# Three reorderings in a two-block sequence kernel: a weight piece converted one step earlier, a residual loaded in four parts, and two projections swapped

## The chip, the cores and the metric

One NeuronCore of a Trainium2 chip runs the whole program in one launch. The metric is device microseconds, lower is better. The kernel before takes 1913.19 us (median of three runs, 1912.94 to 1916.48).

## The reference

The input is 512 tokens of width 1024. The first block runs two layers; each layer scales and shifts its input by a conditioning vector, projects it, runs two recurrent branches (HGRN2 and RWKV7) beside a gate projection, merges them and adds a residual. The second block is one RG-LRU layer and one retention layer. What the change touches is this (cut down):

```
for l in range(2):                                   # first block
    y_hg = o_hg @ w_branch_hg[l];  y_rw = o_rw @ w_branch_rw[l]
    merged = y_hg * sigmoid(gate[0:1024]) + y_rw * sigmoid(gate[1024:2048])
    x = layer_norm(DN_ALPHA * x + (1 + ...) * (merged @ w_out[l]))   # the layer residual x
# RG-LRU layer of the second block
xb = conv4(h @ w_x) + b ;  gate = h @ w_g            # 12 blocks of 128 columns each
a, u = gates(xb);  hseq = scan(a, u);  y = hseq * silu(gate)
```

## The kernel before

Everything is kept transposed, channels on 128 partitions and the 512 tokens along the free dimension. All weights are one list of **pieces** (231 of them, 512 KB each: eight 128x128 tiles). A product in 32 bit is made of three matmuls on rounded parts, so each piece goes through a fixed chain:

- SyncE (SP) loads it into one of two raw buffers (`load_block`, L571), when GpSimd is done with the piece two before it;
- ScalarE (ACT) makes the rounded part `w_hi` (`weights(b)`, L806), when the load has landed and TensorE has used piece b-2;
- GpSimd (POOL) makes the rest `w_lo`, in two instructions of 128x512 (L719);
- TensorE (PE) multiplies, 24 matmuls a piece (L2344 for one output tile, L2363 for four side by side).

Activations are split likewise: a **high part** on ACT (`high`, L814, which waits until VectorE has made the source) and a low part on VectorE (DVE; `low`, L1405). PE waits for both before it uses a tile. The order on each engine is written by hand; each engine works through its own list in order, and semaphores tie the lists together.

**The branch stage** (once for each of the two layers) has eight pieces, b_br to b_br+7: four for the HGRN2 output and four for the RWKV7 output, two pieces for each half of the output columns. PE handles a piece in two steps. Its step for the third RWKV7 tile waits for the low part of that tile and for the first half of w_lo of piece b_br+5, the sixth. DVE makes the four RWKV7 tiles in `normed_head(j)` (four instructions each, L1405 and L1843); `normed_head(3)` also holds the low part of tile 2. ACT meanwhile makes four sigmoids of the gates (`gates(n)`, L1113, 128x2048 each). DVE then scales the residual (L1878) before `merge(0)`; PE's results of the first RWKV7 half are read there. SP loads the 4 MB of gates and then the 2 MB residual x.

**The RG-LRU stage** starts with four convolved blocks x0 to x3, projected side by side into four PSUM banks; after that every block (x for a convolved one, g for a recurrent gate one) goes in turn into one of two PSUM banks, proj0 and proj1, in the order of `LRU_ORDER`. PE may start block n only when the bank of block n-2 has been read. An x block is read by a plain copy on ACT into one of two staging buffers, and DVE convolves it from there (one TENSOR_SCALAR at L1996, three SCALAR_TENSOR_TENSOR at L1408). A g block is read last by DVE: ACT makes its sigmoid into the staging buffer (L1204), and DVE multiplies that with the bank (L1405), which frees it. `staged_before` makes ACT wait until the staging buffer has been convolved.

## Time and profile before

| what | value |
|---|---|
| median of three runs | 1913.19 us (1912.94 to 1916.48) |
| the profiled execution | 1914.83 us, span 1913.0 us |
| PE busy | 1826.5 us, 95% of the span |
| DVE busy | 1101.1 us, 58% |
| ACT busy | 816.8 us, 43% |
| POOL busy | 702.3 us, 37% |
| mean granted TensorE clock | 0.982 |

The span is the time between the first and the last recorded instruction; the execution's own time is 1.83 us more. All times in rows are microseconds from the start of the span unless marked ns.

### The profile page before, as it was taken

What the parts mean: (1) busy time and instruction counts of PE and PEld (TensorE: products, weight loads), DVE (VectorE), ACT (ScalarE), POOL (GpSimd) and SP (SyncE); (2) the same over time, 40 slices, a digit from 0 to 9 for tenths busy, and PEclk for the clock granted to TensorE, in tenths of its full rate; (3) what the DMA queues carried; (4) which work ended last, traced back from release to release, by engine and by line L of the source; (5) the groups of instructions that cost most, each with busy time, mean ns of one, the idle gap of its engine ahead of it and who ended that gap; (6) DMA issues with size and microseconds to landing.
All of it is one profiled execution on the core that took longest, in us unless ns stands there. A gap on an engine that the chain in (4) does not pass through costs nothing.

```text
span 1913.0 us, 35599 instructions
## 1 busy us (share of the span) xinstructions
PE 1826.5 (95%) x14714; PEld 1453.3 (76%) x14714; DVE 1101.1 (58%) x1431; ACT 816.8 (43%) x1173; POOL 702.3 (37%) x488
## 2 busy tenths in 40 slices
PE   7999999999998999999999997899998999999996
PEld 4778877899775877777899784775676888888875
DVE  7775787633455118787633453658845446546454
ACT  2343645533533443755533534345724324323332
POOL 2454433210252435643210251333453435343332
PEclk9998999999998999999999999999998999999998
DMA  9782222200431522222200432322143322222222
GB/s 366 237 258 71 88 95 93 80 26 4 166 99 44 172 83 83 88 94 89 84 26 4 166 99 88 143 67 66 56 143 123 108 60 84 67 78 72 71 99 99
DMA packets 63201, 193.24 MB, mean 101 GB/s; under 512 B 5936, under 2 KB 6192, under 8 KB 62672
## 3 DMA queue, kind: packets, MB, share of 16 engines
q1 hardware_dynamic: 63056, 191.10, 30.3%
q8 instruction: 116, 1.90, 0.4%
q14 instruction: 29, 0.24, 0.0%
HBM read 173.25 MB, written 17.83 MB: 100 GB/s over the span
## 4 chain that ended last, share of the span: by engine, by line
PE 62%; issue 21%; DVE 7%; POOL 7%; ACT 2%; DMA 0%; POOLq 0%; SPq 0%; DVEq 0%; ACTq 0%
PE proj L2344 39%; POOL w_lo_sb L719 6%; PE aux L2363 4%; PE aux L2602 3%; DVE slots_sb L1405 2%; PE proj L2602 1%; PE aux L2517 1%; PE aux L2659 1%; DVE area_sb L1405 1%; PE aux L2656 1%; PE aux L2962 1%; PE aux L2968 1%; PE aux L2374 1%; PE aux L2959 1%; DVE slots_sb L1408 1%
## 5 line engine op out<-in xcount | busy, mean ns | idle before, releaser
L719 POOL TENSOR_TENSOR w_lo_sb<-w_raw_sb,w_hi_sb 128x512 fp32r<-128x512 f32 x462 | 684.6, 1503 | 1033.3 <-ACT w_hi_sb L806 1033.2
L2344 PE MATMUL proj<-act_hi_sb,w_hi_sb 128*128 128x512 f32 x1480 | 604.0, 408 | 14.9 <-POOL w_lo_sb L719 3.4
L2344 PE MATMUL proj<-act_hi_sb,w_lo_sb 128*128 128x512 f32 x1480 | 579.3, 391 | 0.0
L2344 PE MATMUL proj<-act_lo_sb,w_hi_sb 128*128 128x512 f32 x1480 | 578.3, 391 | 0.0
L806 ACT ACTIVATE w_hi_sb<-w_raw_sb 128x1024 fp32r<-128x1024 f32 x231 | 244.5, 1058 | 673.0 <-PE proj L2344 516.2
L2344 PEld LDWEIGHTS proj<-act_hi_sb,w_hi_sb 128*128 128x128 f32 x1480 | 279.1, 189 | 98.3 <-issue 30.6
L2344 PEld LDWEIGHTS proj<-act_lo_sb,w_hi_sb 128*128 128x128 f32 x1480 | 279.4, 189 | 63.0 <-issue 8.9
L2344 PEld LDWEIGHTS proj<-act_hi_sb,w_lo_sb 128*128 128x128 f32 x1480 | 278.9, 188 | 60.1
L2363 PE MATMUL aux<-act_hi_sb,w_hi_sb 128*128 128x512 f32 x336 | 137.7, 410 | 23.3 <-issue 18.2
L1405 DVE TENSOR_TENSOR area_sb<-area_sb 128x256 f32<-128x256 f32 (+1 forms) x180 | 117.7, 698 | 44.4 <-PE aux L2518 28.2
L2363 PE MATMUL aux<-act_lo_sb,w_hi_sb 128*128 128x512 f32 x336 | 133.5, 397 | 0.0
L2363 PE MATMUL aux<-act_hi_sb,w_lo_sb 128*128 128x512 f32 x336 | 133.4, 397 | 0.0
L1405 DVE TENSOR_TENSOR slots_sb<-slots_sb 128x512 f32<-128x512 f32 (+1 forms) x67 | 84.4, 1262 | 42.3 <-ACT slots_sb L1109 22.6
L1405 DVE TENSOR_TENSOR slots_sb<-proj,const_sb 128x512 f32<-128x512 f32 x44 | 30.4, 691 | 118.5 <-PE proj L2344 118.2
L2363 PEld LDWEIGHTS aux<-act_hi_sb,w_hi_sb 128*128 128x128 f32 x336 | 65.0, 193 | 42.6 <-issue 24.5
L1405 DVE TENSOR_TENSOR area_sb<-area_sb,slots_sb 128x512 f32<-128x512 f32 (+1 forms) x90 | 83.5, 946 | 17.8 <-ACT slots_sb L828 11.3
L2363 PEld LDWEIGHTS aux<-act_lo_sb,w_hi_sb 128*128 128x128 f32 x336 | 64.9, 193 | 15.1 <-issue 1.9
L2363 PEld LDWEIGHTS aux<-act_hi_sb,w_lo_sb 128*128 128x128 f32 x336 | 64.6, 192 | 13.9
L2659 PE MATMUL aux<-area_sb 64*64 64x64 f32 x1280 | 71.9, 218 | 0.4 <-issue 0.2
L2602 PE MATMUL aux<-area_sb 64*64 64x64 f32 x1792 | 68.8, 219 | 3.1 <-issue 2.1
L1408 DVE SCALAR_TENSOR_TENSOR slots_sb<-proj,derived_sb,stage_sb 128x512 f32<-128x512 f32 x24 | 18.0, 751 | 93.2 <-ACT stage_sb L876 93.2
L2602 PEld LDWEIGHTS aux<-area_sb 64*64 64x64 f32 x1792 | 63.8, 135 | 4.3 <-issue 2.7
(310 smaller groups left out, 2557.8 us busy)
## 6 DMA issues: line engine op xcount, KB each, us to landing
w_raw_sb<-wall SPq DMA_DIRECT2D x231, 512.0 KB, 3.6
area_sb<-w_ada SPq DMA_DIRECT2D x32, 512.0 KB, 4.5
slots_sb<-w_ada SPq DMA_DIRECT2D x32, 256.0 KB, 6.9
gate_scr<-stage_sb SPq DMA_DIRECT2D x32, 256.0 KB, 2.2
area_sb<-gate_scr SPq DMA_DIRECT2D x8, 1024.0 KB, 9.7
x_scr<-area_sb SPq DMA_DIRECT2D x3, 2048.0 KB, 7.7
area_sb<-x_scr SPq DMA_DIRECT2D x2, 2048.0 KB, 13.5
area_sb<-lru_gates SPq DMA_DIRECT2D x1, 3584.0 KB, 11.7
```

The lines of the kernel that those rows point to most:

```text
L719: nc.gpsimd.tensor_tensor(w_lo[:, b % 2, :, :].rearrange("p k n -> p (k n)")[:, half], w_raw[:, b % 2, half], w_hi[:, b % 2, :, :].rearran ...
L806: A(w_hi[:, b % 2, :, :].rearrange("p k n -> p (k n)"), w_raw[:, b % 2, :], ACT.Copy)\
L1405: return TT(out_ap, a, b, op)
L1408: return STT(out=out_ap, in0=in0, scalar=scalar, in1=in1, op0=op0, op1=op1)
L2344: ins = MM(bank, w[:, s, k, :], a[:, t, :], start=(start and i == 0), stop=(stop and i == len(terms) - 1))
L2363: ins = MM(bank, w[:, s, 4 * (k % 2) + i, :], a[:, t, :], start=(k == 0 and n == 0), stop=(k == len(tiles) - 1 and n == 2))
L2374: return nc.tensor.transpose(dst, src, C("ident"))
L2517: MM(x[0:64, early], a[:, early], b[:, early], start=True, stop=True)
L2602: ins = MM(x[q, columns * j:columns * j + columns], a[q, j, :], b(q, j), start=(i == 0), stop=(i == len(products) - 1))
L2656: MM(x[q, 64 * j:64 * j + 64], xt[q, j, :], z[q, j, :], start=True, stop=True)
L2659: ins = MM(x[q, at:at + 64], z[q, j, :], xt[q, j, :], start=True, stop=True)
L2959: ins = MM(x, r_vtok[:, c, vs], r_scores[:, cols], start=True, stop=(c == 0))
```

## The change

Three orders are changed; no arithmetic is.

1. ACT converts piece b_br+5 before it makes the high part of RWKV7 tile 3, in both layers.
2. The residual of each layer is loaded in four parts of 512 KB. Ahead of each part stands the load of one more weight piece (b_br+4 to b_br+7), so a part can be issued only when that piece's raw buffer is free. DVE waits for all four parts where it waited for the one load.
3. The list of RG-LRU blocks begins with g0, x4 instead of x4, g0, on ACT, DVE and PE, and in the order of the pieces.

```
-LRU_ORDER = [("x", 4), ("g", 0), ("g", 1), ("x", 5), ("g", 2), ...
+LRU_ORDER = [("g", 0), ("x", 4), ("g", 1), ("x", 5), ("g", 2), ...
...
                 src = x_scr[0] if l else dram["x_t"]
-                sp.dma_start(xa[:, :, :], src.rearrange("k p t -> p k t")).then_inc(S("x_in"), 16)
+                for i in range(4):
+                    blocks_to(b_br + 5 + i)
+                    sp.dma_start(xa[:, 2 * i:2 * i + 2, :], src[2 * i:2 * i + 2].rearrange("k p t -> p k t"))\
+                        .then_inc(S("x_in"), 16)
...
                 high_rw(2)
+                weights(b_br + 5)
                 high_rw(3)
-                weights(b_br + 5)
                 gates(2)
                 gates(3)
...
-                dve.wait_ge(S("x_in"), 16 + 16 * l)
+                dve.wait_ge(S("x_in"), 64 + 64 * l)
...
+            lru_block("g", 0)
             lru_block("x", 4)
-            lru_block("g", 0)
             lru_block("g", 1)
```

The last piece of the diff stands on ACT and on DVE, and PE's list begins likewise; later waits on `x_in` count the six additional loads.

**On ACT in the branch stage**, from the high parts of tiles 0 and 1 (first row) to the conversion of piece b_br+7 (last row). L806 and L809 are `weights`, L814 and L817 `high`, L1113 and L1116 `gates`. Before:

```order
L814 ACTIVATE act_hi_sb<-slots_sb 128x512 [waits split_src] x2
L806 ACTIVATE w_hi_sb<-w_raw_sb 128x1024 [waits block_used,raw_in1]
L1113 ACTIVATE area_sb<-area_sb 128x2048 [waits gate_in1]
L814 ACTIVATE act_hi_sb<-slots_sb 128x512 [waits split_src] x2
L806 ACTIVATE w_hi_sb<-w_raw_sb 128x1024 [waits block_used,raw_in0]
L1113 ACTIVATE area_sb<-area_sb 128x2048 [waits gate_in2]
L1113 ACTIVATE area_sb<-area_sb 128x2048 [waits gate_in3]
L806 ACTIVATE w_hi_sb<-w_raw_sb 128x1024 [waits block_used,raw_in1]
L806 ACTIVATE w_hi_sb<-w_raw_sb 128x1024 [waits block_used,raw_in0]
```

The same place of the changed kernel, up to the last gates:

```order
L817 ACTIVATE act_hi_sb<-slots_sb 128x512 [waits split_src] x2
L809 ACTIVATE w_hi_sb<-w_raw_sb 128x1024 [waits block_used,raw_in1]
L1116 ACTIVATE area_sb<-area_sb 128x2048 [waits gate_in1]
L817 ACTIVATE act_hi_sb<-slots_sb 128x512 [waits split_src]
L809 ACTIVATE w_hi_sb<-w_raw_sb 128x1024 [waits block_used,raw_in0]
L817 ACTIVATE act_hi_sb<-slots_sb 128x512 [waits split_src]
L1116 ACTIVATE area_sb<-area_sb 128x2048 [waits gate_in2]
L1116 ACTIVATE area_sb<-area_sb 128x2048 [waits gate_in3]
```

The conversion stands between the two high parts now; the gates and the conversion of b_br+6 still come behind the second of them.

**On SP behind the loads of the gates** in layer 0, the changed kernel has these rows; L571 is `load_block`, L680 a part of the residual:

```order
L675 DMA area_sb<-gate_scr 128x4x512 x3
L571 DMA w_raw_sb<-wall 128x1024 [waits lo_ready]
L680 DMA area_sb<-x_t 128x2x512
L571 DMA w_raw_sb<-wall 128x1024 [waits lo_ready]
L680 DMA area_sb<-x_t 128x2x512
L571 DMA w_raw_sb<-wall 128x1024 [waits lo_ready]
L680 DMA area_sb<-x_t 128x2x512
L571 DMA w_raw_sb<-wall 128x1024 [waits lo_ready]
L680 DMA area_sb<-x_t 128x2x512
```

Before, the row behind the gates was one load of x, 128x8x512, which waited for nothing, and the weight loads followed.

**On DVE at the start of the RG-LRU blocks**, from the convolution of x3 on. L1996 with L1408 x3 is one convolution, a L1405 with `proj` among its inputs frees the bank of a g block. Before:

```order
L1996 TENSOR_SCALAR slots_sb<-stage_sb,vec_sb 128x512 [waits aux_read3]
L1408 SCALAR_TENSOR_TENSOR slots_sb<-stage_sb,vec_sb,slots_sb 128x512 [waits dve_chain] x3
L1996 TENSOR_SCALAR slots_sb<-stage_sb,vec_sb 128x512 [waits proj_read1]
L1408 SCALAR_TENSOR_TENSOR slots_sb<-stage_sb,vec_sb,slots_sb 128x512 [waits dve_chain] x3
L1405 TENSOR_TENSOR slots_sb<-proj,stage_sb 128x512 [waits sig_staged] x2
```

And in the changed kernel, where the same helpers stand three lines further down:

```order
L1999 TENSOR_SCALAR slots_sb<-stage_sb,vec_sb 128x512 [waits aux_read3]
L1411 SCALAR_TENSOR_TENSOR slots_sb<-stage_sb,vec_sb,slots_sb 128x512 [waits dve_chain] x3
L1408 TENSOR_TENSOR slots_sb<-proj,stage_sb 128x512 [waits sig_staged]
L1999 TENSOR_SCALAR slots_sb<-stage_sb,vec_sb 128x512 [waits proj_read0]
L1411 SCALAR_TENSOR_TENSOR slots_sb<-stage_sb,vec_sb,slots_sb 128x512 [waits dve_chain] x3
L1408 TENSOR_TENSOR slots_sb<-proj,stage_sb 128x512 [waits sig_staged]
```

The multiplication for g0 stands between the convolutions of x3 and x4 now. The first bank of the blocks belongs to g0 instead of x4, so it is freed by this DVE instruction, where ACT's copy of x4 freed it before.

## Rows read from the trace of the kernel before

**Rows 1.** The page, busy time of each engine.

```profile
PE 1826.5 (95%) x14714; PEld 1453.3 (76%) x14714; DVE 1101.1 (58%) x1431; ACT 816.8 (43%) x1173; POOL 702.3 (37%) x488
```

**Rows 2.** Timeline, PE, branch stages: start, duration, work, idle before and its releaser.

```profile
523.46 0.39 PE L2363 MATMUL aux<-act_hi_sb,w_lo_sb 128*128 128x512 f32 x1
525.68 0.50 PE L2363 MATMUL aux<-act_hi_sb,w_hi_sb 128*128 128x512 f32 x1 [1.83 <-POOL w_lo_sb L719]
...
531.25 0.39 PE L2363 MATMUL aux<-act_hi_sb,w_hi_sb 128*128 128x512 f32 x1
...
1099.90 0.50 PE L2363 MATMUL aux<-act_hi_sb,w_hi_sb 128*128 128x512 f32 x1 [1.45 <-POOL w_lo_sb L719]
```

**Rows 3.** Timeline, ACT, branch stage of layer 0.

```profile
519.45 0.64 ACT L814 ACTIVATE act_hi_sb<-slots_sb 128x512 fp32r<-128x512 f32 x1 [3.43 <-DVE slots_sb L1405]
522.69 0.63 ACT L814 ACTIVATE act_hi_sb<-slots_sb 128x512 fp32r<-128x512 f32 x1 [2.60 <-DVE slots_sb L1405]
523.23 1.04 ACT L806 ACTIVATE w_hi_sb<-w_raw_sb 128x1024 fp32r<-128x1024 f32 x1
524.18 3.71 ACT L1113 ACTIVATE area_sb<-area_sb 128x2048 f32<-128x2048 f32 x2
527.79 1.05 ACT L806 ACTIVATE w_hi_sb<-w_raw_sb 128x1024 fp32r<-128x1024 f32 x1
```

**Rows 4.** Timeline, POOL, branch stage of layer 0.

```profile
509.05 1.29 POOL L719 TENSOR_TENSOR w_lo_sb<-w_raw_sb,w_hi_sb 128x512 fp32r<-128x512 f32 x1 [6.64 <-ACT w_hi_sb L806]
...
524.35 1.28 POOL L719 TENSOR_TENSOR w_lo_sb<-w_raw_sb,w_hi_sb 128x512 fp32r<-128x512 f32 x1 [7.51 <-ACT w_hi_sb L806]
...
528.91 1.29 POOL L719 TENSOR_TENSOR w_lo_sb<-w_raw_sb,w_hi_sb 128x512 fp32r<-128x512 f32 x1 [2.03 <-ACT w_hi_sb L806]
```

**Rows 5.** Timeline, DVE, branch stage of layer 0.

```profile
509.12 1.76 DVE L1405 TENSOR_TENSOR slots_sb<-slots_sb 128x512 f32<-128x512 f32 x1
...
521.24 0.69 DVE L1405 TENSOR_TENSOR slots_sb<-slots_sb 128x512 f32<-128x512 f32 x1
...
522.58 0.68 DVE L1405 TENSOR_TENSOR act_lo_sb<-slots_sb,act_hi_sb 128x512 fp32r<-128x512 f32 x1
...
526.36 2.67 DVE L1878 TENSOR_SCALAR area_sb<-area_sb 128x4096 f32<-128x4096 f32 x1
```

**Rows 6.** Timeline, SP: issues of x and of piece b_br+7.

```profile
492.02 2.17 SPq L678 DMA_DIRECT2D area_sb<-x_t  x1
...
527.06 0.33 SPq L571 DMA_DIRECT2D w_raw_sb<-wall  x1
```

**Rows 7.** The page, DMA issues: count, KB each, us from issue to landing.

```profile
w_raw_sb<-wall SPq DMA_DIRECT2D x231, 512.0 KB, 3.6
...
area_sb<-x_t SPq DMA_DIRECT2D x1, 2048.0 KB, 17.4
```

**Rows 8.** Timeline, PE, the first matmuls of g1 and of x5.

```profile
1234.35 0.47 PE L2344 MATMUL proj<-act_hi_sb,w_hi_sb 128*128 128x512 f32 x1 [2.56 <-ACT stage_sb L1202]
...
1242.65 0.47 PE L2344 MATMUL proj<-act_hi_sb,w_hi_sb 128*128 128x512 f32 x1 [0.96 <-DVE slots_sb L1405]
```

**Rows 9.** Timeline, ACT, the RG-LRU stage.

```profile
1233.61 0.60 ACT L1202 ACTIVATE stage_sb<-proj 128x512 f32<-128x512 f32 x1 [2.15 <-DVE slots_sb L1408]
```

**Rows 10.** Timeline, DVE: convolution of x3, then the multiplication of g0.

```profile
1233.44 1.48 DVE L1996 TENSOR_SCALAR slots_sb<-stage_sb,vec_sb 128x512 f32<-128x512 f32 x1
...
1235.74 1.65 DVE L1408 SCALAR_TENSOR_TENSOR slots_sb<-stage_sb,vec_sb,slots_sb 128x512 f32<-128x512 f32 x1
...
1241.82 0.68 DVE L1405 TENSOR_TENSOR slots_sb<-proj,stage_sb 128x512 f32<-128x512 f32 x1
```

**Rows 11.** Windows, PE: window, length, busy (instructions), granted clock, DMA share, GB/s.

```profile
1235.20:1238.60 3.40, 3.40 (x10) 0.51 0.51 154
...
1371.90:1375.00 3.10, 3.06 (x7) 0.50 0.24 34
...
1181.80:1187.60 5.80, 5.80 (x8) 0.52 0.00 0
```

More of the change, by code:

```diff
@@ L35 @@
 RET_LOG = [math.log(1.0 - 2.0 ** (-5.0 - h)) for h in range(RET_HEADS)]
-LRU_ORDER = [("x", 4), ("g", 0), ("g", 1), ("x", 5), ("g", 2), ("x", 6), ("g", 3), ("x", 7), ("g", 4), ("x", 8),
+LRU_ORDER = [("g", 0), ("x", 4), ("g", 1), ("x", 5), ("g", 2), ("x", 6), ("g", 3), ("x", 7), ("g", 4), ("x", 8),
              ("x", 9), ("g", 5), ("x", 10), ("g", 6), ("x", 11)] + [("g", j) for j in range(7, 12)]
@@ L2039, in low_y @@
                 low(SPLITS["lru_y"] + t, (t + 8) % RT, G_S[:, t, :])
+            lru_block("g", 0)
             lru_block("x", 4)
-            lru_block("g", 0)
             lru_block("g", 1)
@@ L2117, in _ @@
             dve.wait_ge(S("rms_rs"), 2)
-            dve.wait_ge(S("x_in"), 48)
+            dve.wait_ge(S("x_in"), 144)
             def ret_low(m):
@@ L2317, in _ @@
                 evacuated(dve, RET_OUT + KT + m)
-            onto_x(1, "post1", 8, 112, S("x_final"))
+            onto_x(1, "post1", 8, 208, S("x_final"))
         @block.tensor
@@ L2866, in lru_blocks @@
                     used(project(lru_piece(half, j)))
-            lru_blocks(("x", 4), ("g", 0), ("g", 1), ("x", 5), ("g", 2), ("x", 6))
+            lru_blocks(("g", 0), ("x", 4), ("g", 1), ("x", 5), ("g", 2), ("x", 6))
             pe.wait_ge(S("lru_w"), 16)
```

## The prediction

> **What bounds the kernel now.** I read the page first: TensorE (PE) is busy 95% of the span [rows 1]. So an edit is worth what it takes from or adds to the moments in which PE stands still, and I went through PE's timeline at the three places. In the branch stage PE waits once in each layer, 1.83 us in layer 0 and 1.45 us in layer 1, both times for GpSimd's half of `w_lo` of piece b_br+5 [rows 2]. At the start of the RG-LRU blocks it waits 2.56 us before g1, for ACT's copy of x4, and 0.96 us before x5, for DVE's multiplication of g0 [rows 8]. Behind the first of these waits the granted clock is 0.51 for 3.4 us, that is the lower level, 1.2 GHz for 2.4 [rows 11]. Work behind each place starts from PE, so I let a shift there run through to the end.
>
> **Part 1, the earlier conversion.** ACT makes the high part of tile 2 at 519.45, and has to wait until 522.69 for the source of tile 3; the conversion of b_br+5 follows at 523.23, 0.54 later, and GpSimd begins at 524.35, 1.12 later still [rows 3, 4]. In the new order the conversion starts at 519.45 + 0.54 = 519.99 and GpSimd at 521.11. The first half of w_lo would be there by 522.4, before PE gets to its step: PE's last matmul ahead of the wait starts at 523.46 [rows 2]. By that alone the whole wait goes.
>
> But PE's step also needs the low part of tile 2, which DVE makes at the end of `normed_head(3)`, from 522.58 for 0.68 [rows 5]. Now GpSimd works beside that head. Its price is in the trace: a DVE TENSOR_TENSOR with both inputs in SBUF that starts at 509.12, just behind a GpSimd subtraction of 509.05 for 1.29, takes 1.76 us; one with nothing beside it (521.24) takes 0.69 [rows 4, 5]. The first of the head's last two multiplications starts at 521.24, 0.13 behind GpSimd's new start, and the second meets the second subtraction. Each is 1.07 longer, together 2.1. The low part then starts at 524.7 and is done at 525.4, and PE starts at about 525.4, where it started at 525.68. Of 1.83 us some 0.3 is gained.
>
> The Trainium skill (SBUF — State Buffer, section on the port rules for engines) states that VectorE and GpSimd share a port pair as an exclusive lock, that a VectorE instruction with two SBUF inputs is blocked by a GpSimd one that reads SBUF, and that it is blocked for the whole of it. The 1.76 us agree with that.
>
> Then comes what stands behind the late high part of tile 3. It waits for that head and moves from 522.69 to 524.8. The two gates follow 0.54 later, at 525.33, and take 3.61 to the next conversion [rows 3]; b_br+6 is converted at 528.94 instead of 527.79, and GpSimd begins on it at 530.06 instead of 528.91 [rows 4]. PE's two steps took from 525.68 to 531.25, 5.57 us [rows 2], so now they end at 530.97, and the next step needs GpSimd's first half: 530.06 + 1.29 = 531.35 with nothing beside it. That is 0.15 us later than 531.25, the lower bound.
>
> The upper bound comes from the scaling of the residual on DVE. It stood at 526.36 for 2.67, of which some 2.15 is its own, since GpSimd's two subtractions from 524.35 end at about 526.9 [rows 4, 5]. All of DVE is 2.1 later, so it starts at 528.5 if x is there, ends at 530.65 and, if a GpSimd instruction waits as long as a DVE one does, holds the first half of b_br+6 until 531.9: PE 0.7 later. This comes again in layer 1, where the wait is the same one [rows 2].
>
> **Part 2, the residual in four loads.** Before, x was issued at 492.02 and landed 17.4 us later, at 509.4, so 17 us before DVE wants it [rows 6, 7]. It hid completely, and no weight load was late for it: ACT's conversions there wait for none. The split can gain nothing. Now the last part stands behind the load of b_br+7, which waits for GpSimd to finish b_br+5. That was issued at 527.06 [rows 6]; with GpSimd 2.9 earlier (its second half waits for DVE once) it is about 524.4, and the last part of x goes out at 524.8. A load of 512 KB lands after 3.6 us [rows 7], which is 528.4; with the weight load ahead of it on the same engines, 6 MB in some 20 us being 1.7 us for 512 KB, it is 530.1. DVE wants it at 528.5. If x comes at 529.3, the middle, the scaling ends at 531.45, and GpSimd's half at 532.7: PE 1.5 later. At worst x comes just ahead of GpSimd's start, the scaling runs from 530.0 to 532.15, and PE is 2.2 later; if it comes after, GpSimd is first and the loss falls to 0.2 to 0.7. I take 1.3 us for each layer, between 0.7 and 1.5 but nearer to the latter as x is likelier late than not. Both layers: +2.6 (0.3 to 4.4). Extra issues on SP, 0.33 each [rows 6], delay no load that is waited for.
>
> **Part 3, g0 ahead of x4.** PE may start g1 when the bank of the first block is read. Before, that was ACT's copy of x4 at 1233.61, which only had to wait for the convolution of x2 [rows 9]. Now it is DVE's multiplication of g0, behind the convolution of x3. That one begins at 1233.44; its TENSOR_SCALAR takes 1.48 beside GpSimd, and its second SCALAR_TENSOR_TENSOR, from 1235.74, takes 1.65 [rows 10] where it would take 0.75 alone (an estimate: two more such instructions in the same convolution differ by the same 0.9 us with and without GpSimd). GpSimd comes 1.3 later here, since ACT loads the sigmoid's table and makes g0's sigmoid ahead of that conversion. So the second takes 0.75, to 1236.5, and the third meets GpSimd's start within some hundredths: it ends at 1237.3, or at 1238.35 if GpSimd is first. With 0.68 for the multiplication [rows 10] PE starts g1 at 1238.1 or 1239.2, instead of 1234.35 [rows 8].
>
> From there to x5, before: 1242.65 - 1234.35 = 8.3, of which 1.7 is the low clock (3.4 us at half speed, [rows 11]) and 0.96 the second wait [rows 8]; 5.6 is the block itself. After: the second wait is gone, as the bank of x4 is read by then. PE has stood still for over 6 us, and I expect the clock at its lower level when it starts. After other long waits it stayed there for 3.1 and for 5.8 us of work [rows 11]; half of that is 1.55 to 2.9, and I take 2.0. So x5 starts at 1238.1 + 5.6 + 2.0 = 1245.7 or at 1246.8, that is 3.0 or 4.1 later. I take +3.3; bounds 2.6 and 5.0.
>
> The Trainium skill (TensorE: Matmul & The Clock Gate, "HAM oscillation — how this bites in real kernels") warns that waits of PE between groups of matmuls put the array back at its low clock, so that a wait costs more than its length. The 0.51 behind 2.56 us of waiting agrees.
>
> **Sum.** 2.6 + 3.3 = 5.9 us. On the profiled execution's own time, 1914.83, that is 1920.7. That execution is 1.64 above the median of the three, 1913.19, so against the median it is 1919.1.
>
> **The rivals.**
> - *No measurable change* (24%). The POOL subtraction wins against the scaling in both layers and x is not late (+0.2 each, or a gain of 0.3 each), and the RG-LRU term is at its low end, 2.6: 1915 to 1917. For it: these are orders of a few hundredths. Against it: the clock, which has fallen in every longer wait that I looked at.
> - *Faster* (6%). The wait in the blocks is only moved: DVE works without a break for long stretches later in the RG-LRU stage, and a stall shared with those would be paid once. The delay is then taken up, the second wait and the low clock are gone (0.96 + 1.7), and the conversion gives both waits in full (1.83 + 1.45): -5.9, 1907.3. It decides if x5 starts no later than 1242.65. Against it: g1 cannot start before the convolution of x3 ends, and 1237.3 + 5.6 is past 1242.65 without any low clock.
> - *Slower by more* (in the 70% for slower, about 12%). PE's new wait for b_br+6 passes 2.5 us in both layers, and the clock falls there as it did behind 2.56 us: 1.7 more each, 1922.5 to 1924.
> - *The conversion does what it says* (within the others, 15%): if DVE's head is not held, the waits go in full, -3.3, and with the RG-LRU term nothing is left: 1913.2.
>
> **How the numbers follow.** Forecast 1919.1, slower by 0.31%. What a measurement of this kernel can tell from no change is 0.2%, 3.8 us. Terms at their bounds give +2.9 to +9.4; with the case of unheld heads the lower end reaches 1913.2, of which I leave out the last part: 1914.5 to 1923.0. Faster 0.06, same 0.24, slower 0.70.
>
> **What would show it.** Part 1: PE's wait for `w_lo` before tile 3 replaced by a shorter one for DVE's `act_lo`, two multiplications of 1.7 us on DVE, and a new PE wait of 1 to 2 us some 5.5 us later. Part 2: DVE's scaling preceded by a wait for the x DMA. Part 3: a single PE wait of 6 to 7 us before g1, and none before x5. I am wrong if DVE and GpSimd do not hold each other there, or if the clock comes back at once.

## The result

The changed kernel took 1921.27 us (median of 7 executions, 1918.9 to 1922.03), the kernel before in the same session 1913.78 us (7 executions, 1911.55 to 1917.35). The ratio is 1.0031, with a 95% interval of 1.002 to 1.0042: slower by 0.3%, about 6 us. The two medians themselves lie further apart, 7.5 us or 0.39%, which is inside that interval.

**Stretch by stretch.** The two profiled executions span 1913.0 and 1920.2 us (the latter is the slowest of its seven), and I cut both at six moments that exist in each. The timeline of PE after the change has them as follows (start, duration, work, idle before and its releaser): the first matmul of the branch stage of layer 0, the end of that stage in the layer norm, the same two of layer 1, the first matmul of the RG-LRU stage, and the first behind a wait that stands late in that stage.

```profile
489.31 1.13 PE L2771 MATMUL aux<-slots_sb,const_sb 128*128 128x512 f32 x2 [0.48 <-ACT slots_sb L1040]
...
600.79 0.70 PE L2803 MATMUL aux<-area_sb,const_sb 128*128 128x512 f32 x1 [0.91 <-DVE area_sb L1411]
...
1065.42 0.70 PE L2771 MATMUL aux<-slots_sb,const_sb 128*128 128x512 f32 x1 [0.48 <-ACT slots_sb L1040]
...
1173.49 1.10 PE L2388 MATMUL aux<-stage_sb,const_sb 128*128 128x512 f32 x2 [1.54 <-ACT stage_sb L824]
...
1201.37 0.58 PE L2366 MATMUL aux<-act_hi_sb,w_hi_sb 128*128 128x512 f32 x1 [5.02 <-issue]
...
1325.02 0.47 PE L2347 MATMUL proj<-act_hi_sb,w_hi_sb 128*128 128x512 f32 x1 [1.60 <-DVE slots_sb L1408]
```

Before, these moments were 489.47, 599.13, 1064.06, 1168.77, 1197.02 and 1317.78; the wait at the last of them was 1.60 us there too. The differences give this table, in us. All later ones are in it as well, so that each experiment can be read from it; "change" is the kernel with all three parts.

| kernel | branch 0 | between | branch 1 | between | RG-LRU | rest | span |
|---|---|---|---|---|---|---|---|
| before | 109.66 | 464.93 | 104.71 | 28.25 | 120.76 | 595.22 | 1913.0 |
| after (the change) | 111.48 | 464.63 | 108.07 | 27.88 | 123.65 | 595.18 | 1920.2 |
| e1, part 1 alone | 110.42 | 464.93 | 105.43 | 27.51 | 120.36 | 595.15 | 1909.9 |
| e2, part 2 alone | 109.75 | 466.14 | 104.73 | 27.67 | 120.50 | 595.14 | 1913.4 |
| e3, part 3 alone | 109.69 | 465.60 | 105.01 | 27.97 | 123.70 | 595.26 | 1920.0 |
| e4, change, no collision | 108.90 | 464.69 | 104.17 | 27.42 | 124.80 | 595.13 | 1917.4 |
| e5, part 1, next piece earlier | 109.38 | 465.81 | 104.41 | 28.41 | 120.84 | 595.07 | 1915.4 |
| e7, both convolved blocks first | 111.30 | 465.78 | 105.06 | 27.50 | 119.62 | 595.25 | 1913.8 |
| e8, e7 and filler | 111.34 | 465.88 | 105.01 | 27.62 | 119.70 | 595.28 | 1915.0 |
| e9, change and long filler | 110.93 | 465.83 | 106.23 | 27.18 | 128.93 | 595.33 | 1926.2 |
| e10, e7 and filler to size | 109.67 | 464.73 | 104.73 | 28.15 | 120.05 | 595.30 | 1910.3 |
| e11, change and filler to size | 111.22 | 464.71 | 106.37 | 28.43 | 122.73 | 595.18 | 1920.2 |
| e12, branch stage reordered | 109.05 | 466.81 | 104.08 | 27.91 | 119.69 | 595.48 | 1913.7 |
| e13, e12 and five fillers | 109.05 | 464.59 | 104.09 | 26.19 | 118.19 | 595.36 | 1904.8 |

What is missing to the span is the time ahead of the first moment. It lay between 486.1 and 492.8 us in these executions, although no kernel here changes anything in it. So the span of one execution tells nothing about an edit of 1 us, and the stretches do. Where two kernels have the same code, branch stages, RG-LRU stretches and the rest differ by 0.6 us at most, with two exceptions: a branch stage in which the clock falls, which the experiments come to, and the RG-LRU stretch of e4. In branch 1 nearly all of the spread between kernels with the code of before (104.71 to 105.06) has one origin: some 26 us into that stage GpSimd's second subtraction and a multiplication on DVE start within some hundredths of each other. Where GpSimd is first (e3, e7, e8), the multiplication takes 1.83 instead of 0.69 us and PE's later wait is 1.75 instead of 1.45. In before, the changed kernel and all others the multiplication took 0.68 or 0.69 us, so their branches 1 can be compared to about 0.1 us. The stretches between are looser, 464.6 to 466.8 and 27.2 to 28.4 us.

The change adds 1.82 us in branch 0, 3.36 in branch 1 and 2.89 in the RG-LRU stretch. With -0.16 ahead of them, -0.30 and -0.37 between and -0.04 behind, that is the 7.2 us between the two spans.

**The branch stage after.** The timeline of PE, at the two places of [rows 2]:

```profile
525.22 0.47 PE L2366 MATMUL aux<-act_hi_sb,w_hi_sb 128*128 128x512 f32 x1 [1.54 <-DVE act_lo_sb L1408]
...
532.75 0.50 PE L2366 MATMUL aux<-act_hi_sb,w_hi_sb 128*128 128x512 f32 x1 [1.83 <-POOL w_lo_sb L722]
...
1100.97 0.47 PE L2366 MATMUL aux<-act_hi_sb,w_hi_sb 128*128 128x512 f32 x1 [1.16 <-DVE act_lo_sb L1408]
...
1108.43 0.51 PE L2366 MATMUL aux<-act_hi_sb,w_hi_sb 128*128 128x512 f32 x1 [1.76 <-POOL w_lo_sb L722]
```

The one wait has become two. The first is shorter than before by 0.29 in both layers (1.83 and 1.45 in [rows 2]) and is now for DVE's low part; the second, for GpSimd's half of b_br+6, did not exist. From the start of the stage to the matmul behind the second wait it is 532.75 - 489.31 = 43.44 us, and it was 531.25 - 489.47 = 41.78 [rows 2]: 1.66 longer. In layer 1 the same works out at 1.60.

DVE's timeline shows the held instructions and then the wait for x:

```profile
521.07 1.71 DVE L1408 TENSOR_TENSOR slots_sb<-slots_sb 128x512 f32<-128x512 f32 x1
522.82 1.66 DVE L1408 TENSOR_TENSOR slots_sb<-slots_sb 128x512 f32<-128x512 f32 x1
524.40 0.68 DVE L1408 TENSOR_TENSOR act_lo_sb<-slots_sb,act_hi_sb 128x512 fp32r<-128x512 f32 x1
...
529.28 2.29 DVE L1881 TENSOR_SCALAR area_sb<-area_sb 128x4096 f32<-128x4096 f32 x1 [1.02 <-DMA area_sb<-x_t]
```

And GpSimd's timeline shows what held them, and what it was held by in turn:

```profile
520.94 1.29 POOL L722 TENSOR_TENSOR w_lo_sb<-w_raw_sb,w_hi_sb 128x512 fp32r<-128x512 f32 x1 [4.28 <-ACT w_hi_sb L809]
522.19 1.73 POOL L722 TENSOR_TENSOR w_lo_sb<-w_raw_sb,w_hi_sb 128x512 fp32r<-128x512 f32 x1
529.77 2.93 POOL L722 TENSOR_TENSOR w_lo_sb<-w_raw_sb,w_hi_sb 128x512 fp32r<-128x512 f32 x1 [5.84 <-ACT w_hi_sb L809]
```

The two multiplications of `normed_head(3)` take 1.71 and 1.66 us where an undisturbed one takes 0.69 [rows 5]. The scaling starts at 529.28, 0.49 ahead of GpSimd's subtraction, and that one takes 2.93 us instead of 1.29. PE starts 0.05 us after it is done.

The windows of PE behind the new wait of layer 1 (window, length, busy and instructions, granted clock, DMA share, GB/s) show one thing more:

```profile
1105.00:1108.00 3.00, 1.66 (x8) 1.00 0.00 0
1109.20:1112.60 3.40, 3.40 (x10) 0.53 0.38 90
1112.80:1115.00 2.20, 2.20 (x11) 0.99 0.39 88
```

For 3.4 us TensorE ran at its lower level, 1.2 GHz. That is nearly all of what branch 1 has lost beyond the 1.60: 3.36 - 1.60 = 1.76 us. In layer 0 no such stretch follows the wait of 1.83, and there 1.82 - 1.66 = 0.16 us is lost behind the wait all the same; in e1, e9 and e11 it is 0.13 to 0.17. So the low clock itself cost about 1.6.

**The RG-LRU stage after.** PE's timeline has one wait instead of the two of [rows 8]:

```profile
1243.12 0.77 PE L2347 MATMUL proj<-act_hi_sb,w_hi_sb 128*128 128x512 f32 x1 [7.27 <-DVE slots_sb L1408]
```

The timelines of GpSimd and of DVE show how near the race was, and the windows of PE show the clock ahead of and behind the wait:

```profile
1240.57 1.26 POOL L722 TENSOR_TENSOR w_lo_sb<-w_raw_sb,w_hi_sb 128x512 fp32r<-128x512 f32 x1 [1.87 <-ACT w_hi_sb L809]
```

```profile
1240.59 1.79 DVE L1411 SCALAR_TENSOR_TENSOR slots_sb<-stage_sb,vec_sb,slots_sb 128x512 f32<-128x512 f32 x1
1242.30 0.68 DVE L1408 TENSOR_TENSOR slots_sb<-proj,stage_sb 128x512 f32<-128x512 f32 x1
```

```profile
1239.50:1243.00 3.50, 0.00 (x0) 0.50 0.53 150
1243.20:1246.30 3.10, 3.10 (x8) 0.56 0.53 143
1246.60:1249.00 2.40, 2.40 (x12) 1.00 0.05 12
```

GpSimd was first by 0.02 us, so the convolution's last instruction took 1.79, which is the later of the two cases of the forecast. PE's g1 starts 1243.12 - 1201.37 = 41.75 us behind the stage's first matmul; counted from before's 1197.02 that is 1238.8, where 1239.2 was given for this case and [rows 8] has 1234.35. The granted clock is already 0.50 while PE waits, and stays low for the first 3.1 us of work.

### The profile page after: what moved, and what is told of

Its sections match the earlier page's. It is cut to its first block, busy times and chain, and to the rows that moved or that the text cites. A ratio compares the mean times of both kernels' runs of the same rounds, so it can differ in the third digit from the quotient of the medians.

```text
span 1920.2 us, 35573 instructions
## 1 busy us (share of the span) xinstructions
PE 1827.4 (95%) x14714; PEld 1454.0 (76%) x14714; DVE 1107.0 (58%) x1431; ACT 816.0 (42%) x1173; POOL 705.9 (37%) x488
## 4 chain that ended last, share of the span: by engine, by line
PE 62%; issue 22%; DVE 7%; POOL 7%; ACT 2%; DMA 0%; POOLq 0%; SPq 0%; DVEq 0%; ACTq 0%
PE proj L2347 39%; POOL w_lo_sb L722 7%; PE aux L2366 4%; PE aux L2605 3%; DVE slots_sb L1408 2%; PE proj L2605 1%; PE aux L2520 1%; PE aux L2662 1%; DVE area_sb L1408 1%; PE aux L2659 1%; PE aux L2965 1%; PE aux L2971 1%; PE aux L2377 1%; PE aux L2962 1%; DVE slots_sb L1411 1%
## 5 line engine op out<-in xcount | busy, mean ns | idle before, releaser
L809 ACT ACTIVATE w_hi_sb<-w_raw_sb 128x1024 fp32r<-128x1024 f32 x231 | 244.3, 1058 | 683.0 <-PE proj L2347 517.4
L1408 DVE TENSOR_TENSOR area_sb<-area_sb 128x256 f32<-128x256 f32 (+1 forms) x180 | 117.7, 697 | 44.4 <-PE aux L2521 28.2
L1408 DVE TENSOR_TENSOR slots_sb<-slots_sb 128x512 f32<-128x512 f32 (+1 forms) x67 | 88.4, 1322 | 42.2 <-ACT slots_sb L1112 22.5
L1408 DVE TENSOR_TENSOR slots_sb<-proj,const_sb 128x512 f32<-128x512 f32 x44 | 30.4, 690 | 118.6 <-PE proj L2347 118.2
L1408 DVE TENSOR_TENSOR area_sb<-area_sb,slots_sb 128x512 f32<-128x512 f32 (+1 forms) x90 | 83.4, 945 | 17.8 <-ACT slots_sb L831 11.3
```

What stands on the lines that cost most here:

```text
L809: A(w_hi[:, b % 2, :, :].rearrange("p k n -> p (k n)"), w_raw[:, b % 2, :], ACT.Copy)\
L1408: return TT(out_ap, a, b, op)
```

## The experiments

Diffs of e1, e2, e3, e5, e7 and e12 are against the kernel before, those of e4, e9 and e11 against the changed kernel. Medians are set beside those of the kernel before in the same session (25 to 33 executions).

### e1, e2, e3: each part alone

Each is the kernel before with one part of the diff shown ahead: `weights(b_br + 5)` ahead of `high_rw(3)` (e1), the four loads of x with their counts (e2), or g0 ahead of x4 on ACT, DVE and PE and in `LRU_ORDER` (e3).

e1 was expected to do this:

> The kernel before with part 1 alone (b_br+5 converted ahead of the high part of tile 3, both layers). My theory (DVE and GpSimd hold each other): DVE's last two multiplications of normed_head(3) take about 1.7 us each instead of 0.69; PE's wait before tile 3 is no longer for w_lo but for DVE's act_lo, 1.2 to 1.5 us instead of 1.8 and 1.5; a new PE wait for w_lo of about 1 us comes 5.6 us later; PE is 0.7 us later than before behind each branch stage (the residual is there in time here). Total +1.4 us, within -0.5 to +3. Rival (the conversion does what it says, and the loss comes from the other parts): both PE waits gone, total -3.3 us.

e2:

> The kernel before with part 2 alone (residual in four loads). My theory: DVE waits some 5 us for the last part, because it is issued behind the load of b_br+7 at about 527.5 us and lands 4.6 us later, but PE is not delayed: the merged tiles have some 5 us to spare. No new PE wait in the branch stage, total 0 within 1 us. Rival (the split costs by itself): the late scaling delays the merged tiles or holds a subtraction of GpSimd that PE waits for, +1 us or more for each layer, +2 to +3 in all.

e3:

> The kernel before with part 3 alone (g0 ahead of x4). My theory: one PE wait of 7 to 7.5 us before g1, none before x5, the low clock for 1.5 to 3 us at half speed's cost behind it; x5 starts 2.9 us later than before; total +2.9 us, within +2 to +4. Rival (the delay is taken up further on, where DVE works without a break): the waits at 1317 and 1372 us of the kernel before shrink, total 0 to +1 us.

Measured: e1 1915.66 against 1916.10 us, ratio 0.9999 (0.9985 to 1.0012); e2 1915.77, ratio 0.9999 (0.9988 to 1.0009); e3 1919.65, ratio 1.0016 (1.0005 to 1.0027). By the table, e1 adds 0.76 and 0.72 us to the branch stages, e2 adds 0.09 and 0.02, and e3 adds 2.94 to the RG-LRU stretch. The branch sums of e1 and e2, 1.48 and 0.11 us, are below what these medians can tell; the stretches of the profiled executions can tell them.

PE and DVE of e1, from their timelines:

```profile
522.05 0.47 PE L2363 MATMUL aux<-act_hi_sb,w_hi_sb 128*128 128x512 f32 x1 [1.55 <-DVE act_lo_sb L1405]
```

```profile
517.90 1.71 DVE L1405 TENSOR_TENSOR slots_sb<-slots_sb 128x512 f32<-128x512 f32 x1
...
525.00 2.28 DVE L1878 TENSOR_SCALAR area_sb<-area_sb 128x4096 f32<-128x4096 f32 x1
```

The held head comes from part 1 alone: same 1.71, same wait of 1.55. The scaling waits for no load here and starts 7.10 us behind that multiplication; in the changed kernel it is 8.21. And it is 2.28 long against a GpSimd that comes 1.60 later, so it holds that one for 0.7 us only.

DVE of e2, from its timeline:

```profile
532.09 2.29 DVE L1881 TENSOR_SCALAR area_sb<-area_sb 128x4096 f32<-128x4096 f32 x1 [5.64 <-DMA area_sb<-x_t]
```

Here DVE stands 5.64 us waiting for the last part of x, and the stage is no longer for it. So a late x is hidden by itself; the two parts together lose what neither loses alone. In branch 0 the change costs 1.82, and e1 and e2 together 0.76 + 0.09 = 0.85: the missing 1.0 us is their interaction. In layer 1, without the 1.76 that came with the low clock, it is 1.60 against 0.74. The loss grows with the lateness of x. DVE waits for it 0, 0.46, 0.78 and 1.02 us in branch 0 of e1, e9, e11 and the changed kernel, and these stages are 0.76, 1.27, 1.56 and 1.82 us longer than before: nearly microsecond for microsecond.

### e4: the collision taken away from the changed kernel

GpSimd's subtractions for b_br+5 cover 8 columns of 512 here, so the kernel leaves out most of the low part of that piece.

```
+            def low_small(b):
+                pool.wait_ge(hi_ready, b + 1)
+                for at in (0, HALF):
+                    (the subtraction of low(b) for the 8 columns [at:at + 8])
...
+                low_blocks(at, first["branch", l] + 5)
+                low_small(first["branch", l] + 5)
+                at = first["branch", l] + 6
```

> The changed kernel, but GpSimd's two subtractions for piece b_br+5 cover 8 columns of 512 each in both layers (so most of the low part of that piece is left out of the product). All waits stay. My theory (the two engines hold each other): DVE's last two multiplications of normed_head(3) take 0.7 us each again, the PE wait before tile 3 is gone in both layers, and of the new wait for b_br+6 at most 1 us is left; against the changed kernel -2.5 us for each layer, -5 us in all (-3.5 to -7 with the clock). Rival (DVE is late for another reason, such as ACT's conversion ahead of the high part): the multiplications stay near 1.7 us or the wait before tile 3 stays above 1 us, and the total is within 1 us of the changed kernel.

Measured: 1917.99 us, ratio to the kernel before 1.0008 (0.9998 to 1.0019); against the changed kernel branch 0 is 2.58 shorter and branch 1 3.90. DVE's two multiplications beside the short GpSimd work, from its timeline:

```profile
524.09 0.69 DVE L1419 TENSOR_TENSOR slots_sb<-slots_sb 128x512 f32<-128x512 f32 x1
524.82 0.69 DVE L1419 TENSOR_TENSOR slots_sb<-slots_sb 128x512 f32<-128x512 f32 x1
```

They are back at 0.69, and PE has no wait before tile 3 any more. What remains is a wait of 1.00 us (0.93 in layer 1) for the half of b_br+6, and no low clock behind it. Without GpSimd's work beside the head the stages are 0.76 and 0.54 shorter than before, so the whole price of the change there stands behind that work (some of it by way of x, whose last part is also issued earlier when GpSimd is done sooner: DVE waits 0.36 us for it here). The RG-LRU stretch was 124.80 here, 1.15 more than after, with the low clock through some 10 us of 1234 to 1245. PE's wait before g1 is the same 7.27 us, but the work behind it ran at the low level for longer, by PE's windows:

```profile
1239.00:1244.60 5.60, 5.60 (x13) 0.50 0.33 97
1244.80:1249.00 4.20, 4.20 (x20) 1.00 0.00 0
```

That is 5.6 us of work, where it was 3.1 in the changed kernel. Half of the additional 2.5 us is 1.25, so the difference is the clock's. Why the low level lasted longer in the same code is open.

### e5: the next piece converted ahead of the gates too

```
                 high_rw(2)
+                weights(b_br + 5)
                 high_rw(3)
-                weights(b_br + 5)
+                weights(b_br + 6)
                 gates(2)
                 gates(3)
-                weights(b_br + 6)
                 weights(b_br + 7)
```

> The kernel before with part 1, and with piece b_br+6 converted ahead of the last two gates. Measured from the start of a branch stage to its first wait in the layer norm, where the kernel before takes 109.66 and 104.71 us and part 1 alone 110.42 and 105.43. My theory (the new wait comes from ACT's order: the gates stand ahead of that conversion, and DVE's scaling holds GpSimd): the wait for act_lo stays near 1.5 and 1.2 us, the new wait for w_lo is gone, and the stages take 109.4 and 104.4 us. Rival (GpSimd is late for another reason, such as the load of the piece): a wait for w_lo over 0.5 us stays and the stages take 110.2 and 105.2 us or more.

Measured: 1914.78 against 1915.40 us, ratio 0.9992 (0.9978 to 1.0005). The waits of 1.54 and 1.16 for `act_lo` stay and the wait for b_br+6 is gone; the stages are 0.28 and 0.30 shorter than before (branch 1 of e5 is one of those that compare to 0.1 us). This is the gain of 0.3 from the held head, seen alone: the forecast's first step for part 1 holds, and the loss is all in what comes behind it.

### e7, e8, e10: can the RG-LRU waits be had?

e7 puts x4 and x5 first on all three engines:

```
-            lru_blocks(("x", 4), ("g", 0), ("g", 1), ("x", 5), ("g", 2), ("x", 6))
+            lru_blocks(("x", 4), ("x", 5), ("g", 0), ("g", 1), ("g", 2), ("x", 6))
```

> The kernel before with the list x4, x5, g0, g1, g2 instead of x4, g0, g1, x5, g2. From the first matmul of the RG-LRU stage to PE's wait of 1.6 us at 1317.8 the kernel before takes 120.76 us, the changed one 123.65. My theory (what counts is that the banks of the first two blocks are freed by copies on ACT and not by multiplications on DVE): the wait of 2.56 us before the third block stays, the wait of 0.96 us before the fourth is gone, and the stretch takes 119.8 us, 1.0 us less. Rival (DVE's total work sets the pace there): the wait only moves to a later block, and the stretch takes 120.7 us or more.

Measured: 1914.76 against 1915.40 us, ratio 0.9995 (0.9984 to 1.0006). The wait of 0.96 us for DVE's multiplication is down to 0.17 and stands a block later, the one before the third block stays (2.55), and the stretch is 119.62, 1.14 shorter. But branch 0, whose code is that of before, took 111.30 instead of 109.66. PE's windows in it:

```profile
526.60:529.80 3.20, 3.20 (x9) 0.51 0.49 164
530.20:533.00 2.80, 2.80 (x14) 1.00 0.26 39
```

Its wait at 525.53 is 1.84 us, and behind it the clock is low. In the kernel before it is 1.83 [rows 2], and the windows there read thus:

```profile
526.40:529.80 3.40, 3.40 (x17) 1.00 0.46 140
```

So the same wait in the same code brings the low clock in one execution and not in another, and it costs 111.30 - 109.66 = 1.64 us where it does. The branch 0 of e8 is a second such case (wait 1.82, low clock, 111.34), those of e3 and e10 are cases without (waits 1.83 and 1.84, clock 1.00, 109.69 and 109.67).

e8 fills the wait that stays with matmuls of constants, whose result nobody reads, between x5 and g0:

```
+            for _ in range(5):
+                MM(aux[5][:, :], C("ones"), C("scan64"), start=True, stop=True)
```

> The one before, and 5 matmuls of constants into a free bank while PE waits for the third block (their result is overwritten unread). They take some 2.2 of the 2.56 us. My theory (the granted clock falls because PE stands still, and that is paid in the next block): no low clock behind this wait, the third block takes 5.6 instead of 7.3 us, the stretch takes 118.1 us, 1.7 us less than without them. Rival (the low clock has another cause, or the filler delays the block): the stretch stays at 119.8 us or grows by the filler.

Measured: 1915.27 us, ratio 1.0 (0.999 to 1.001), stretch 119.70. I had mis-sized it: a matmul of 512 such columns takes 0.86 us, so five took 4.3, 1.7 longer than the wait. The low clock was gone and the overrun cost what the clock gave. e10 has the filler at 1408 columns:

```
+            def filler(name, columns):
+                x = job_open(pe, name)
+                while columns > 0:
+                    n = min(columns, 512)
+                    MM(x[:, 0:n], C("ones"), C("scan64", 0, n), start=True, stop=True)
+                    columns -= n
...
+            lru_blocks(("x", 4), ("x", 5))
+            filler(("lru_gate", 0, 5), 1408)
+            lru_blocks(("g", 0), ("g", 1), ("g", 2), ("x", 6))
```

> As the kernel with x4 and x5 first and a filler, but the filler has 1408 columns of constants in place of 2560: in the last runs 512 columns took 0.86 us, so this is 2.36 us in the 2.56 us wait, where the old one took 4.3 and ran 1.7 us over. My theory (PE's standing still brings the low clock): no low clock behind the place, the third block starts no later than without the filler, the stretch from the start of the RG-LRU stage to the 1.6 us wait takes 118.0 us instead of 119.6. Rival (the filler itself delays PE, or DVE sets the pace): 119.5 us or more.

Measured: 1914.22 against 1915.84 us, ratio 0.9997 (0.9985 to 1.0009), stretch 120.05. The timeline of PE and its windows:

```profile
1232.27 0.47 PE L2351 MATMUL proj<-act_hi_sb,w_hi_sb 128*128 128x512 f32 x1 [0.20 <-ACT stage_sb L1202]
...
1245.30 0.47 PE L2351 MATMUL proj<-act_hi_sb,w_hi_sb 128*128 128x512 f32 x1 [1.71 <-DVE slots_sb L1405]
```

```profile
1231.00:1235.00 4.00, 3.81 (x16) 1.00 0.28 68
```

The filler fits the wait to 0.20 us and the clock is 1.00 behind it. The 1.7 us that the low clock cost come back two blocks later as a wait of 1.71 for DVE. This stretch is paced by DVE: while PE ran slowly, DVE caught up, and that time was not lost. Of the 1.7 us expected of the clock nothing is seen (120.05 against e7's 119.62).

### e9, e11: the changed kernel with its long wait filled

e9 puts 15 matmuls of 512 columns between x4 and g1 of the changed kernel, e11 `filler(("lru_gate", 0, 5), 4160)` in the same place.

> The changed kernel with 15 matmuls of constants into a free bank while PE waits for g1 (7.27 us there). My theory: part 3 costs 2.9 us because of the longer wait and of the clock behind it; with PE busy the clock stays up, g1 takes 5.6 us, and the stretch from the start of the RG-LRU stage to the 1.6 us wait takes 122.1 us instead of 123.65; it stays above the 120.76 of the kernel before. Rival (the clock has no part in it): 123.6 us.

> As the changed kernel with a filler, but 4160 columns, 7.0 us in the 7.27 us wait before g1. My theory: no low clock behind it, g1 takes 5.6 us, the stretch takes 122.1 us instead of 123.65, and so 1.3 us of the 2.9 that part 3 costs are left without any clock effect. Rival (the clock has no part): 123.6 us or more.

Measured: e9 1926.75 against 1915.40 us, ratio 1.0059 (1.0042 to 1.0076), stretch 128.93; its filler took 12.9 us for a wait of 7.27, by the same error in size as in e8. e11 1919.54 against 1915.84 us, ratio 1.0021 (1.001 to 1.0033), stretch 122.73. PE of e11, from its timeline:

```profile
1237.01 7.20 PE L2332 MATMUL aux<-const_sb 128*128 128x512 f32 x18
...
1244.45 0.47 PE L2354 MATMUL proj<-act_hi_sb,w_hi_sb 128*128 128x512 f32 x1 [0.23 <-DVE slots_sb L1408]
```

The clock is 1.00 behind it, and the stretch 0.92 shorter than after. So 122.73 - 120.76 = 2.0 us of part 3 is there without the low clock. What the low clock adds is better counted from g1 on, since g1 starts 41.75 us into the stretch after and 42.16 in e11: from there to the end it is 81.90 and 80.57, so 1.3 us, and by the same count 83.27 - 80.57 = 2.7 in e4. All are read from single executions. e9 and e11 carry a second reading. Their branch stages are those of the changed kernel, and no low clock fell behind the wait for b_br+6 in either, 1.69 us in layer 1 of e11: branch 1 is 106.23 and 106.37, that is 1.5 and 1.7 above before. That is the local 1.60 without the clock.

### e12: the branch stage in another order

```
                 high_rw(2)
-                high_rw(3)
                 weights(b_br + 5)
                 gates(2)
                 gates(3)
+                high_rw(3)
                 weights(b_br + 6)
...
                 normed_head(2)
+                low(SPLITS["rw", l] + 2, 2, P3[:, 2, :])
+                gated_hg(1)
                 normed_head(3)
                 low(SPLITS["rw", l] + 3, 3, P3[:, 3, :])
-                gated_hg(1)
-                dve.wait_ge(S("x_in"), 16 + 16 * l)
-                chain.done(TS(xa[:, :, :], xa[:, :, :], DN_ALPHA, None, ALU.mult))
                 merge(0)
                 merge(1)
+                dve.wait_ge(S("x_in"), 16 + 16 * l)
+                chain.done(TS(xa[:, :, :], xa[:, :, :], DN_ALPHA, None, ALU.mult))
```

It carries e7's order of the blocks as well, and the condition `if j:` ahead of the low part in `normed_head` becomes `if j in (1, 2):`.

> The kernel before with x4 and x5 first, and another order in the branch stage: ACT converts b_br+5, then makes the last two gates, then the high part of tile 3; DVE makes the low part of tile 2 at once, then gates the second half of the HGRN2 output (its inputs are in PSUM), then normed_head(3), and scales the residual behind the merge. My theory (GpSimd holds DVE only where both inputs of DVE are in SBUF): GpSimd's subtractions for b_br+5 run beside the gating and hold it little; PE's wait of 1.8 us before tile 3 is gone, one of 1.3 us for the low part of tile 3 takes its place 2.7 us later; branch stages of 109.0 and 104.0 us instead of 109.66 and 104.71. Rival (any order that moves the conversion pays for it in full): 109.6 and 104.7 or more. RG-LRU stretch 119.7 us.

Measured: 1913.58 against 1915.84 us, ratio 0.9989 (0.9978 to 1.0). The branch stages are 0.61 and 0.63 shorter than before, the RG-LRU stretch 1.07. GpSimd and DVE, from their timelines:

```profile
522.33 1.30 POOL L719 TENSOR_TENSOR w_lo_sb<-w_raw_sb,w_hi_sb 128x512 fp32r<-128x512 f32 x1 [4.28 <-ACT w_hi_sb L806]
```

```profile
523.14 0.68 DVE L1405 TENSOR_TENSOR area_sb<-area_sb,proj 128x512 f32<-128x512 f32 x1
```

GpSimd now works beside the gating, whose second input is in PSUM (`proj`, `aux`), and this is not held: 0.68. The same shape with two inputs in SBUF took 1.71. So it matters which of DVE's work the conversion lies beside, and not only how early it comes. That GpSimd holds DVE only where both inputs are in SBUF is too narrow, though: the scaling of x is a TENSOR_SCALAR with one tensor from SBUF, and it took 2.67 us beside GpSimd's subtraction [rows 5] and 2.29 alone. And e12 changes more than this one neighbour: the scaling of x goes behind the merge as well, so its gain belongs to the whole order. PE's wait before tile 3 (1.83) is replaced by one for DVE's low part (1.23), which is that gain of 0.6.

### e13: the same with fillers before five long waits

e12 with e10's filler, and fillers of 4096 columns before layer 1's first matmul, 2944 and 2816 around the sum of squares ahead of the RG-LRU stage, and 3328 before the retention stage.

> The last one with a filler in five waits of PE, each some 0.2 to 0.4 us shorter than the wait: 6.9 us before layer 1, 4.95 us ahead of the squares before the RG-LRU stage, 4.7 us ahead of its first matmul, 2.36 us at its third block, 5.6 us ahead of the retention stage. My theory (the low clock follows PE's waits and is paid in the work behind them): the stretches at the low clock behind these waits vanish; in the kernel before 5.7, 5.9, 4.0, 3.5 and 5.3 us of work lie in them, half of that is 12.2 us. With 1.4 us from the branch stages and 1.0 from x5: 14 us less than before, about 0.7%, within 8 and 16. Rival (fillers take PE's sequencer or run over, or the clock falls elsewhere): less than 4 us.

Measured: 1909.78 us (10 executions, 1906.56 to 1913.3) against 1915.84 (33 executions, 1911.53 to 1918.41), ratio 0.9971 (0.9961 to 0.9981). It is the fastest of all, faster than both kernels. The stretches add up to 6.1 us less than before, where 14 were expected. Set against e12, whose order it shares, the medians differ by 3.8 us: that is what the fillers brought. Behind the first branch stage the low clock is left at two places, from 1364 and from 1466. Where it is gone, waits stand instead, as the first two of these from PE's timeline; behind the third, which before did not have, the clock falls again:

```profile
617.85 0.47 PE L2371 MATMUL aux<-act_hi_sb,w_hi_sb 128*128 128x512 f32 x1 [1.14 <-DVE act_lo_sb L1405]
...
1239.74 0.47 PE L2352 MATMUL proj<-act_hi_sb,w_hi_sb 128*128 128x512 f32 x1 [1.75 <-DVE slots_sb L1405]
...
1466.06 0.50 PE L2371 MATMUL aux<-act_hi_sb,w_hi_sb 128*128 128x512 f32 x1 [2.67 <-POOL w_lo_sb L719]
```

## Why the prediction was right, and where it was not

The forecast was 1919.1 us, slower by 0.31%; measured were 1921.27 us and 0.31% (0.20 to 0.42). That the per cent agree to the last digit is luck: the terms were off in both directions (2.6 forecast and 3.3 shown for the branch stages without the clock, 3.3 and 2.9 for the RG-LRU stage), and the medians lie 0.39% apart.

**Part 1, the head that GpSimd holds: right.** The multiplications took 1.71 and 1.66 us where 1.76 was taken, PE's first wait shrank by 0.29 us where 0.3 was forecast, and e5 shows that gain alone. e1 added 0.76 and 0.72 us, the forecast's 0.7 for a scaling that x does not delay. e4 takes the collision away, and with it the loss; the rival by which the conversion does what it says would need unheld heads and falls. The Trainium skill (SBUF — State Buffer, "Who interferes with whom") has it that a VectorE instruction with at most one SBUF input, outside its two-port modes, does not contend with GpSimd. The 0.68 us of e12, for an instruction with its other input in PSUM, agree.

**Part 2, the residual in four loads: right in its mechanism, and mis-sized.** Alone it costs nothing (e2), though DVE waits 5.64 us for x. Beside part 1 the scaling started at 529.28, where 529.3 was expected, and it held GpSimd as said: 2.93 us. The term was +1.3 per layer for both parts; it came to 1.66 and 1.60, beyond the 1.5 that I had worked out for x at the middle of its range and short of the 2.2 of the worst case. So the term is mis-sized by 0.3 to 0.4 per layer. Part of it is the scaling itself, 2.29 us where I had taken 2.15 [rows 4, 5]. And I had taken 0.2 off those 1.5 for cases in which GpSimd goes first; in the changed kernel, e9 and e11 the scaling was first in both layers, by 0.49 to 1.06 us.

**The rival "slower by more" came true in one layer.** I had tied it to a wait of 2.5 us. In layer 1 of the changed kernel the clock fell behind 1.76 us and cost about 1.6. The runs together show that the length of this wait does not decide it: the clock fell behind 1.84 (e7), 1.82 (e8) and 1.76 (after), and did not behind 1.84 (e10), 1.83 (before, e3, and layer 0 of after) nor 1.69 (e11). What does decide it is open. Since e9 and e11 have the changed kernel's branch stages without a fall, it belongs to single executions, and how often it comes cannot be told from profiles of one execution for each kernel.

**Part 3, g0 ahead of x4: right.** The forecast was +3.3; the change showed +2.89 and e3 alone +2.94. Its mechanism was that g1 has to wait for DVE's multiplication behind the convolution of x3, and PE waited 7.27 us for just that. By the steps of the forecast, g1 starts 1238.8 - 1234.35 = 4.4 us later (3.8 or 4.9 were given), and the wait before x5 (0.96) and the old low clock (1.7) are gone, which leaves 1.8. The new low clock is then 2.89 - 1.8 = 1.1; e11 finds 1.3. The term for it was 2.0, and this is the one that was mis-sized: work at the low level lasted 3.1 us at 0.56, the short end of what I had read from [rows 11]. In e4, behind the same wait, it lasted 5.6 us and cost 2.7, near the long end. So single executions lie near both ends of the 1.55 to 2.9 that I gave, the changed kernel's own a little below it, and what places them there is open.

**The rival "faster"** stood on the delay being absorbed later in the stage, and fell: the wait at 1325.02 is the same 1.60 us as before, and the rest of the program is as long as it was (595.18 against 595.22). **The rival "no measurable change"** needed GpSimd to win over the scaling in both layers, and it won in neither. Its other half, an RG-LRU term at its low end, came near.

## What to carry to other kernels

To start one engine earlier is to place it beside other work: look up what its partner is doing at the new moment, with which inputs, and whether a partner's instruction of the same form was already twice as long once beside it. In the trace here a neighbour of 0.69 us had a twin of 1.76. A load that is hidden may be moved later for nothing only as long as the engine that waits for it does not hold another when it does run; here the late load was free alone and cost 1 us more beside the earlier conversion. And a low clock is worth removing only where PE sets the pace of the next blocks: of the 12.2 us that the arithmetic of the clock promised for five fillers, 3.8 came (e13 against e12).

## What the runs showed of the hardware

- The granted clock fell behind waits of 1.82 and 1.84 us in two executions (e7, e8) and not behind 1.83 and 1.84 in three others (before, e3, e10), in code that did not differ there; and behind 1.76 in the changed kernel, but not behind 1.69 of the same code in e11. A fall cost 1.6 to 1.7 us where PE set the pace.
- Behind the same wait of 7.27 us the clock stayed low for 3.1 us of work in one execution and for 5.6 in another (after and e4), which made 1.4 us.
- The clock's price can be nothing: taking a low stretch of 3.4 us away gave a wait of 1.71 us for DVE in its place (e10).
- The holding goes both ways, and can cost an instruction more than its own length: GpSimd's subtraction of 1.29 us took 2.93 beside a DVE TENSOR_SCALAR of 2.29 that had started 0.49 earlier.
- Which of the two is held can hang on some hundredths of a microsecond: in branch 1 one such race went one way in three executions and the other way in the rest, and moved PE's wait from 1.45 to 1.75 us.
- A matmul of 512 columns of fp32 constants takes 0.86 us, in e8, where I had counted half.
- The time ahead of the first branch stage differed by 6.7 us between executions of the same code (486.1 to 492.8).
